# A decoder layer on one core: x is turned raw as it lands, and the norm's token factor is applied afterwards, to v and to the turned rows

## What is computed

```python
y = rmsnorm(h, norm_mix[i])              # xf * rsqrt(mean(xf*xf) + eps) * g
q, k, v = jnp.split(y @ w_in, 3, axis=-1)
# one block of 256 keys: s = q k^T * dh**-0.5 + bias[bucket(t - s)], causal; softmax; o = p v
h = h + o @ w_out
h = h + squared_relu_mlp(rmsnorm(h, norm_mlp[i]), mlp_up[i], mlp_down[i])
return rmsnorm(h, final_norm)
```

## Time and profile before

| | us |
|---|---|
| median of 3 runs | 310.87 (310.7 to 311.29) |
| the profiled execution | 310.88 |
| its span in the profile | 309.2 |
| TensorE busy | 299.7 |
| VectorE busy | 205.8 |
| ScalarE busy | 160.0 |

### The profile page before, as it was taken

One profiled execution on the slowest core, in us unless ns is written; L12 is line 12 of the kernel. 1 busy time (PEld: TensorE's weight loads), 2 busy tenths in 40 slices (PEclk: granted clock), 3 DMA queues, 4 the chain that ended last, 5 costly groups with the idle time before them and its releaser, 6 DMA issues.

```text
span 309.2 us, 4658 instructions
## 1 busy us (share of the span) xinstructions
PE 299.7 (97%) x1679; PEld 254.0 (82%) x1679; DVE 205.8 (67%) x397; ACT 160.0 (52%) x293; POOL 9.3 (3%) x17
## 2 busy tenths in 40 slices
PE   7899999999999999999999999999999999999992
PEld 5588879888888888988888888888888888888881
DVE  3696995875884669686495476567558548557564
ACT  4685754854755435665354445447436445544422
POOL 2301000000000000000000000000000000000000
PEclk9999999999999999999999999999999999999999
DMA  6999988146166047366755746656565574620003
GB/s 221 354 282 357 355 282 270 73 137 272 68 187 223 2 142 229 119 174 221 224 185 144 259 148 184 215 164 221 158 199 208 144 238 161 166 105 0 0 3 136
DMA packets 36654, 55.87 MB, mean 181 GB/s; under 512 B 1128, under 2 KB 29840, under 8 KB 36640
## 3 DMA queue, kind: packets, MB, share of 16 engines
q1 hardware_dynamic: 35632, 52.43, 52.9%
q0 software_dynamic: 992, 3.25, 2.9%
q10 hardware_dynamic: 16, 0.00, 0.0%
HBM read 54.61 MB, written 1.07 MB: 180 GB/s over the span
## 4 chain that ended last, share of the span: by engine, by line
PE 90%; DVE 4%; DMA 2%; ACT 1%; issue 1%; SPq 1%; DVEq 0%; ACTq 0%
PE bank L403 36%; PE bank L358 26%; PE bank L359 13%; DMA h_sb<-in_x_dram 2%; PE bank L336 2%; PE bank L337 2%; PE bank L338 2%; PE bank L323 1%; PE bank L379 1%; PE bank L442 1%; PE bank L441 1%; PE bank L393 1%; PE bank L371 1%; DVE w_lo L759 1%; PE bank L369 1%
## 5 line engine op out<-in xcount | busy, mean ns | idle before, releaser
L759 DVE TENSOR_TENSOR w_lo<-raw,w_hi 128x1024 fp32r<-128x1024 f32 x94 | 112.7, 1220 | 58.2 <-ACT w_hi L559 56.2
L358 PE MATMUL bank<-yT,w_hi 128*128 128x512 f32 x368 | 131.6, 400 | 0.1
L559 ACT CAST w_hi<-raw 128x1024 fp32r<-128x1024 f32 x93 | 94.6, 1048 | 56.6 <-PE bank L403 56.6
L359 PE MATMUL bank<-yT,w_lo 128*128 128x256 f32 x368 | 103.2, 280 | 0.0
L358 PEld LDWEIGHTS bank<-yT,w_hi 128*128 128x128 f32 x368 | 69.1, 188 | 17.8 <-issue 1.3
L403 PE MATMUL bank<-w_hi,hT 128*128 128x512 f32 x256 | 71.8, 390 | 0.0
L359 PEld LDWEIGHTS bank<-yT,w_lo 128*128 128x128 f32 x368 | 69.5, 189 | 0.6
L403 PEld LDWEIGHTS bank<-w_hi,hT 128*128 128x128 f32 x256 | 47.0, 188 | 9.7
L403 PE MATMUL bank<-w_lo,hT 128*128 128x512 f32 x128 | 40.2, 390 | 0.0
L403 PEld LDWEIGHTS bank<-w_lo,hT 128*128 128x128 f32 x128 | 24.0, 188 | 5.2
L629 ACT COPY part<-bank 128x256 f32<-128x256 f32 x30 | 11.2, 373 | 23.3 <-PE bank L359 23.3
(11 more groups left out here) (96 smaller groups left out, 247.2 us busy)
## 6 DMA issues: line engine op xcount, KB each, us to landing
raw<-in_mlp_up_dram SPq DMA_DIRECT2D x16, 1024.0 KB, 5.6
raw<-in_mlp_down_dram SPq DMA_DIRECT2D x16, 1024.0 KB, 4.9
raw<-in_a_w_in_dram SPq DMA_DIRECT2D x10, 1024.0 KB, 9.2
raw<-in_a_w_out_dram SPq DMA_DIRECT2D x4, 1024.0 KB, 4.9
bias_sb<-bias_by_distance POOLq DMA_DIRECT2D x4, 512.0 KB, 6.0
raw<-in_a_w_in_dram SPq DMA_DIRECT2D x4, 256.0 KB, 6.0
raw<-in_a_w_in_dram SPq DMA_DIRECT2D x2, 512.0 KB, 8.2
out_dram<-y_sb SPq DMA_DIRECT2D x4, 256.0 KB, 2.4
```

Source lines behind the costliest of these rows:

```text
L358: mm(dst[:], wh[:, k, own], yT[:, k, :, :], start=(k == 0), stop=False, skip_group_check=True)
L359: last = mm(dst[:, 0:T], wl[:, k, own], yT[:, k, HI, :], start=False, stop=(k == KB - 1), skip_group_check=True)
L559: nc.scalar.copy(w_hi[:, slot, part_of], raw[:, slot, part_of]).then_inc(hi_done, 1)
L759: v.tensor_tensor(w_lo[:, slot, own], raw[:, slot, own], f32(w_hi[:, slot, own]), ALU.subtract).then_inc(lo_done, 1)
```

## The change

Raw x is turned instead of scaled rows: `transposes_first` waits for the landing of x alone and reads `h_sb`. `yT_whole` multiplies with the gain as before, so `yF` now lacks the token factor, and `v_first` computes v without it; `v_scaled` on ScalarE puts the factor on v when it copies v out of its bank. For q and k the factor has to stand along the columns of the turned rows, so VectorE makes a diagonal matrix of the factors (`factor_diag`), TensorE multiplies an all-ones matrix with it (`spread_factor`: every row of the bank then holds the 128 factors), and VectorE multiplies `yF` with that into `y_sb`, read as turned rows through `yN` (`yT_scaled`). The hi and lo parts are made from `yN`. All squares are ScalarE's now. FILL goes from 6 to 2, the bias product moves into `v_first(0)`, ahead of the transposes of block 1, which come after the fourth product in place of the sixth. The two bias tables are loaded from ScalarE's queue, ahead of the gain, and the fill table from GpSimd after x has landed. The load of the exponential's table moves behind `v_scaled(1)` and a further split of weights.

```diff
@@ -50,7 +50,7 @@
 PIECES = 4
-FILL = 6
+FILL = 2
...
@@ -187,6 +189,10 @@
+        def yN(ks, tb):
+            return y_sb[:, tb, :].rearrange("p (k n) -> p k n", k=KB)[:, ks, :]
...
@@ -240,13 +246,12 @@
                                     channel_multiplier=1).then_inc(ident_made, 1)
-            nc.gpsimd.dma_start(rel_sb[:], rel_bias).then_inc(tables_loaded, 16)
-            nc.gpsimd.dma_start(onehot_sb[:], bucket_onehot).then_inc(tables_loaded, 16)
+            pool.wait_ge(x_next, 16)
             nc.gpsimd.dma_start(fill_sb[:], causal_fill).then_inc(fill_loaded, 16)
...
                 ks, tok = slice(4 * b, 4 * b + 4), slice(0, P)
-                nc.gpsimd.tensor_tensor(yT[:, ks, LO, tok], yF[:, ks, tok], yT[:, ks, HI, tok].bitcast(F32),
+                nc.gpsimd.tensor_tensor(yT[:, ks, LO, tok], yN(ks, 0), yT[:, ks, HI, tok].bitcast(F32),
...
@@ -275,19 +280,21 @@
-                if tb == 0:
-                    pe.wait_ge(ident_made, 1)
                 for k in range(KB):
-                    if k == 0:
-                        pe.wait_ge(rows0_dve, 2 * tb + 1)
-                    if k == 2 and tb == 0:
-                        pe.wait_ge(rows0_dve, 2)
-                    if k == 4:
-                        pe.wait_ge(rows0_act, tb + 1)
+                    if tb == 0 and k % 4 == 0:
+                        pe.wait_ge(x_half[k // 4], 16)
+                    if tb == 1 and k == 0:
+                        pe.wait_ge(x_next, 16)
                     last = nc.tensor.transpose(bank[FIRST[tb][k]][:, k % 4 * P:(k % 4 + 1) * P],
-                                               y_sb[:, tb, k * P:(k + 1) * P], ident[:])
+                                               h_sb[:, tb, k * P:(k + 1) * P], ident[:])
                     if k in ((1, 3, 7) if tb == 0 else (3, 7)):
                         last.then_inc(yt_done, 1)
+            def spread_factor(tb):
+                pe.wait_ge(diag_done, tb + 1)
+                mm(bank[SPREAD[tb]][:, 0:P], warm[:, 0:P], diag[:, tb, :], start=True, stop=True
+                   ).then_inc(spread_done, 1)
...
@@ -313,8 +320,14 @@
                 for k in range(KB):
-                    if k == 6 and tb == 0:
+                    if k == 4 and tb == 0:
+                        spread_factor(0)
+                        pe.wait_ge(tables_loaded, 32)
+                        mm(bank[BIAS][0:HEADS, 0:BV], rel_sb[:], onehot_sb[:], start=True, stop=True
+                           ).then_inc(bias_summed, 1)
                         transposes_first(1)
+                    if k == 2 and tb == 1:
+                        spread_factor(1)
...
@@ -580,23 +591,23 @@
-            def rows_first(tb):
-                act.wait_ge(rstd_done, tb + 1)
-                nc.scalar.activation(y_sb[:, tb, 512:D], h_sb[:, tb, 512:D], ACT.Copy,
-                                     scale=stat[:, tb, RSTD:RSTD + 1]).then_inc(rows0_act, 1)
             def yT_hi_first(tb, b):
-                act.wait_ge(yf_done, b + 2 if tb == 0 else b + 4)
+                act.wait_ge(yn_done, 2 * tb + b + 1)
                 ks, tok = slice(4 * b, 4 * b + 4), slice(tb * P, (tb + 1) * P)
-                nc.scalar.copy(yT[:, ks, HI, tok], yF[:, ks, tok]).then_inc(yhi_done, 1)
+                nc.scalar.copy(yT[:, ks, HI, tok], yN(ks, tb)).then_inc(yhi_done, 1)
             def yT_hi(tb):
...
                                    bank[NORM[tb][b]][:].rearrange("p (k n) -> p k n", k=4)).then_inc(yhi_done, 1)
+            def v_scaled(tb):
+                act.wait_ge(unit_done, tb + 1)
+                act.wait_ge(rstd_done, tb + 1)
+                nc.scalar.activation(v_sb[:, tb, :], bank[UNIT[tb]][:, 0:CW], ACT.Copy,
+                                     scale=stat[:, tb, RSTD:RSTD + 1]).then_inc(v_ready, 1)
...
@@ -644,33 +655,34 @@
+            nc.scalar.dma_start(onehot_sb[:], bucket_onehot).then_inc(tables_loaded, 16)
+            nc.scalar.dma_start(rel_sb[:], rel_bias).then_inc(tables_loaded, 16)
             nc.scalar.dma_start(mix_rows[:], norm_mix[0].rearrange("(k p) -> k p", p=P)).then_inc(mix_loaded, 16)
...
             act.wait_ge(x_half[1], 16)
-            nc.scalar.activation(squares[:, 1, 0:256], h_sb[:, 0, 512:768], ACT.Square, scale=ROOT,
+            nc.scalar.activation(squares[:, 1, :], h_sb[:, 0, 512:D], ACT.Square, scale=ROOT,
                                  accum_out=stat[:, 0, SS1:SS1 + 1]).then_inc(square0_act, 1)
             norm_root(0, SS1, (square0_act, 2), 1)
-            rows_first(0)
+            act.wait_ge(x_next, 16)
+            act.wait_ge(square0_act, 2)
+            nc.scalar.activation(squares[:].rearrange("p b n -> p (b n)"), h_sb[:, 1, :], ACT.Square, scale=ROOT,
+                                 accum_out=stat[:, 1, SS0:SS0 + 1]).then_inc(square0_act, 1)
+            act.wait_ge(eps_made, 1)
+            norm_root(1, SS0, (square0_act, 3), 1)
             yT_hi_first(0, 0)
-            act.wait_ge(x_next, 16)
-            act.wait_ge(square0_act, 1)
-            nc.scalar.activation(squares[:, 0, :], h_sb[:, 1, 0:512], ACT.Square, scale=ROOT,
-                                 accum_out=stat[:, 1, SS0:SS0 + 1]).then_inc(square0_act, 1)
-            norm_root(1, SS0, (square0_act, 3), 2)
-            rows_first(1)
             yT_hi_first(0, 1)
-            yT_hi_first(1, 0)
             act.wait_ge(q_first, 16)
             nc.scalar.copy(w_hi[:, 1, 0:HALF], raw[:, 1, 0:HALF]).then_inc(hi_done, 1)
+            yT_hi_first(1, 0)
             yT_hi_first(1, 1)
+            v_scaled(0)
+            hi_tile(1, 1)
+            v_scaled(1)
+            hi_tile(2, 0)
             nc.scalar.preload_act_table(ACT.Exp)
-            v_copy(0, 0)
-            hi_tile(1, 1)
-            v_copy(0, 1)
-            hi_tile(2, 0)
...
@@ -810,11 +822,21 @@
-            def rows_first(tb, own):
+            def factor_diag(tb):
+                root_inverse(tb)
                 dve.wait_ge(rstd_done, tb + 1)
-                v.tensor_scalar(y_sb[:, tb, own], h_sb[:, tb, own], stat[:, tb, RSTD:RSTD + 1], None, ALU.mult
-                                ).then_inc(rows0_dve, 1)
+                v.tensor_scalar(diag[:, tb, :], ident[:], stat[:, tb, RSTD:RSTD + 1], None, ALU.mult
+                                ).then_inc(diag_done, 1)
+            def yT_scaled(tb, b):
+                if b == 0:
+                    dve.wait_ge(spread_done, tb + 1)
+                ks, tok = slice(4 * b, 4 * b + 4), slice(tb * P, (tb + 1) * P)
+                per_row = bank[SPREAD[tb]][:, 0:P]
+                spread = bass.AP(tensor=per_row.tensor, offset=per_row.offset,
+                                 ap=[per_row.ap[0], [0, 4], per_row.ap[1]])
+                v.tensor_tensor(yN(ks, tb), yF[:, ks, tok], spread, ALU.mult).then_inc(yn_done, 1)
...
@@ -937,32 +959,25 @@
             v.memset(warm[:], 1.0).then_inc(warm_made, 1)
-            dve.wait_ge(x_half[1], 16)
-            v.tensor_tensor_reduce(y_sb[:, 0, 768:D], h_sb[:, 0, 768:D], h_sb[:, 0, 768:D], 1.0 / D, 0.0,
-                                   ALU.mult, ALU.add, stat[:, 0, SS2:SS2 + 1]).then_inc(square0_dve, 1)
-            dve.wait_ge(square0_act, 1)
-            dve.wait_ge(square0_dve, 1)
-            v.scalar_tensor_tensor(stat[:, 0, PART_VAR:PART_VAR + 1], stat[:, 0, SS0:SS0 + 1], EPS,
-                                   stat[:, 0, SS2:SS2 + 1], ALU.add, ALU.add).then_inc(var_done, 1)
-            root_inverse(0)
-            rows_first(0, slice(0, 256))
-            rows_first(0, slice(256, 512))
+            v.memset(stat[:, 1, PART_VAR:PART_VAR + 1], EPS).then_inc(eps_made, 1)
+            dve.wait_ge(ident_made, 1)
             dve.wait_ge(mix_turned, 1)
             v.tensor_copy(mixT[:], bank[MIX][:, 0:KB]).then_inc(mix_ready, 1)
+            dve.wait_ge(square0_act, 1)
+            v.tensor_scalar(stat[:, 0, PART_VAR:PART_VAR + 1], stat[:, 0, SS0:SS0 + 1], EPS, None, ALU.add
+                            ).then_inc(var_done, 1)
             dve.wait_ge(mix_ready, 1)
...
             yT_whole(0, 4, 4, 3)
-            dve.wait_ge(x_next, 16)
-            v.tensor_tensor_reduce(y_sb[:, 1, 512:D], h_sb[:, 1, 512:D], h_sb[:, 1, 512:D], 1.0 / D, 0.0,
-                                   ALU.mult, ALU.add, stat[:, 1, SS2:SS2 + 1]).then_inc(square0_dve, 1)
-            dve.wait_ge(square0_dve, 2)
-            v.tensor_scalar(stat[:, 1, PART_VAR:PART_VAR + 1], stat[:, 1, SS2:SS2 + 1], EPS, None, ALU.add
-                            ).then_inc(var_done, 1)
-            root_inverse(1)
-            rows_first(1, slice(0, 512))
+            factor_diag(0)
+            yT_scaled(0, 0)
+            yT_scaled(0, 1)
             yT_whole(1, 0, 4, 4)
             yT_whole(1, 4, 4, 5)
+            factor_diag(1)
+            yT_scaled(1, 0)
+            yT_scaled(1, 1)
             lo_tile(1, 0)
...
             yT_lo_first(1)
```

12 lines of the change are left out of this document (6 added, 6 removed).

## The result

The changed kernel takes 312.45 us (median of 13 runs, 311.72 to 313.33), beside 310.93 us for the kernel before (13 runs, 309.81 to 311.29): a ratio of 1.0058, with a 95% interval of 1.0046 to 1.0070. It is slower, by 1.4 to 2.2 us (this interval), and outside the range that was forecast. The profiled execution took 312.30 us with a span of 310.6.

A forecast was written before the change was run, and what follows sets the result against it. TensorE, busy 299.7 of 309.2 us, was taken as the bound; its 1.9 us earlier v work shrinks to 0.55 at the q product and 0.2 at the k unit, giving 310.67 us, range 310.0 to 311.7.

The forecast's parts named there:

- The start on TensorE: TensorE from first transposes through v: 0.22 us a pass, v work ending at 15.9 instead of 17.8, -1.9 us.
- The rival: TensorE's full clock comes late with two idle products, v passes 0.43 us each: 311.6 to 312.7 at 0.18; chance 0.24 overall.
- the small edits: Three DMA issues ahead of ScalarE's table load make its first square 1.0 us later; fill table and other shifts hidden.
- The first gate: First q product on TensorE, released by VectorE's preparation: 17.2 to 17.3 in place of 17.8, -0.55 us.
- The second gate: First k unit, waiting for VectorE to empty its bank after ScalarE's k half: 23.39 to 23.2, -0.2 us.
- the rival on it: ScalarE drains about 1.38 us after the table load: sum +1.2 us, 312.1; chance 0.02.
- rival 1: Tables off GpSimd's queue let x and v land 0.4 us sooner: -0.6 in all, 310.0 to 310.3; chance 0.21.
- The diagonal: VectorE's block 1 diagonal: half or less of 0.49 us, done by 12.0, TensorE asks at 13.0, hidden by 1.0.
- The multiplication and the preparation: VectorE multiplies turned rows with spread factors, 1.29 us a pair; preparation for the q product ends at 17.1, unmoved.

The follow-up runs named there:

- e1: The changed kernel with six idle products in place of two, nothing else; 311.83 us, ratio 1.0044 to the kernel before.
- e4: The kernel before with two idle products instead of six; 311.55 us, ratio 1.0040 to the kernel before.
- e2: The changed kernel with the gain's load first on ScalarE's queue, the two tables behind it, two idle products kept; 311.49 us, ratio 1.0034.
- e5: The changed kernel with six idle products, gain loaded first, exponential's table load moved behind the first half of tile 4; 311.07 us, ratio 1.0022.
- e6: The kernel before with the exponential's table load moved behind the first half of tile 4; 310.68 us, ratio 1.0003.
- e8: The changed kernel with four idle products, gain first, table load late, bias product later, second spread product and second diagonal earlier; 310.12 us, ratio 0.9979.
- changed, again: The changed kernel measured once more without further edits; 312.75 us, ratio 1.0062 to the kernel before.
- e10: The kernel before with bias tables loaded from ScalarE's queue behind the gain, fill table from GpSimd after x landed; 310.26 us, ratio 0.9996.
- e3: The changed kernel with six idle products and the gain loaded first; 311.61 us, ratio 1.0037 to the kernel before.

## Why the prediction was wrong

The direction was wrong: 310.67 was forecast, -0.2 us, and 312.45 came. Its steps, beside what the trace after gives:

| step | forecast | changed kernel | off by |
|---|---|---|---|
| block 0's transposes start | 3.6 | 5.07 | +1.5 |
| third v product | 7.65 | 6.83 + 4 x 0.43 = 8.5 | +0.9 |
| block 1's transposes start | 9.5 | 11.02 | +1.5 |
| v work ends | 15.9 | 14.78 + 2.75 = 17.5 | +1.6 |
| first q product | 17.2 | 18.70 | +1.5 |
| first k product | 23.2 | 24.77 | +1.6 |

**The clock was the step that failed.** The step is the term of 0.22 us a pass for the v passes of block 0, in "The start on TensorE": it supposes the full clock there with two idle products in place of six. The eight passes took (9.96 - 6.83) / 8 = 0.39 us each, 1.3 us more in all. From there to the k product every step of the changed kernel takes what the forecast gave it, within 0.2 us, so that difference is still there at the end. e1 shows the passes back at 0.22 with six idle products, and e4 that the cut in the filling costs the old kernel 1.2 us by itself. The rival had the mechanism and the price (311.7 to 312.7, slower from a rise later than 8.5 us; it rose at 9.65); its chance was too low for what the rows said. They show what TensorE did ahead of the rise, working without a break from 1.27 to 4.35, and the change takes away exactly that. (The forecast gives 4.36 us for this; that is the length of the idle products, and the rise lies inside it.) The forecast also took the full clock without its cost: e1 gets it with six idle products and gives 0.8 us back at the first v pass. That the granted clock read 1.00 in the rows at 4 and 6 us was no evidence for the changed kernel. What the page TensorE: Matmul & The Clock Gate of the Trainium skill says of transposes ("Part 4: PE-mode transpose") stood beside the rival and was left out of its chance: the changed kernel turned x from 5.07 to 7.0 and had the lower level for 2.6 us more, which agrees. e2 fits it less well: with two idle products and the transposes earlier, from 3.49, the clock rose 1.0 us after the first v pass and not 2.8 us after it. No run takes the transposes apart from the rest, so this stays open.

**The gain's load wasn't costed.** Under the small edits the three DMA issues were followed to the squares, and the third of them, the gain, wasn't followed to the turned gain, which is the next thing on TensorE. It was issued at 1.74, and TensorE, which could turn it at 4.90, stood 1.56 us. The transposes behind it started 1.5 us late; the first v pass, by the forecast 7.65 - 0.9 = 6.75, came at 6.83, so the lateness itself was nearly covered, and what it did was to leave TensorE idle ahead of the clock's rise. e2 turned the gain at 3.27.

**The first gate was right in its form.** VectorE's preparation released the q product, as forecast, and TensorE waited 1.17 us for it, forecast 1.3. It follows the second spread product, and this carried the 1.5 us from the first v passes to the q product.

**The second gate was right.** ScalarE's table load between the halves of the k tile was forecast to give away part of the gain; q to k took 6.07, forecast 5.95, and e5 and e6 show it from both sides: 0.45 us back in the changed order, nothing in the old.

**No drain behind the table load.** The load runs 19.55 to 20.83, the instruction ahead of it ends at 19.53, and the next starts at 20.85, as the row of before had it; the rule of the Trainium skill, ScalarE: Activation LUTs, "What ACT_TABLE_LOAD costs", isn't seen in this kernel either, and the rival on it falls.

**The tables' queue: no gain seen.** The sign of rival 1, block 1 of x ahead of 8.8, did not come (8.90), and the filled hole did not bring it. It landed 6.2 us after its issue in the changed kernel, 6.4 before. In the traces of the experiments it took 5.8 and 6.0 us with the tables on GpSimd and 5.0 to 6.1 with them on ScalarE; on one chip alone it ran from 5.1 (e8) to 6.1 (changed, again), both with the tables on ScalarE. The spread from run to run is larger than the 0.4 us in question, and e10 can't exclude them.

**The diagonal was covered, by luck.** It was put at half of 0.49 us with 1.0 us of cover. It took 1.29 us, ended at 14.40, and TensorE, 1.5 us late by the clock, came for it at 14.54. In e3, at the full clock, it ended at 13.19 and TensorE came at 13.25; in e8, with the order changed, the cover did not hold. That VectorE's diagonal would meet GpSimd's subtraction was not in the forecast.

**The multiplication and the preparation were right**: 1.28 us for the pair, by the row of the same form.

What remains between e3 and the kernel before, 1.2 us, isn't shown apart. The order is a likely part: v, spread and bias product stand ahead of block 1's transposes, so that an early landing of x isn't used (in e3 it landed at 8.48 and was turned from 9.73). e8 changes this together with the number of idle products and the second gate, and gains 0.8% on the changed kernel on the same chip (0.6% by the ratios of e3 and e8); how that divides among its parts wasn't tried one by one.

## What to carry to other kernels

Idle products ahead of the first real one are part of the critical path's speed: before they are cut, count what TensorE will do without a break until the clock rises, and price the first products at both levels. When loads are put in a new order on a queue, follow every one of them to its first reader, the small ones too. A shortened chain ends at the next gate: find it before the gain is written down, and mend both.
